# Gate columns of two mixer layers: one f32 product becomes three products of rounded parts, with weights rounded by a converting GpSimd transfer

## The reference, cut to what matters

```python
def hybrid_mixer(h, ...):          # h: 256 x 1024, the normed input
    (aq, ak, av, bq, ...) = jnp.split(h @ w_in, points, axis=-1)
    ya = diff_attention(...); yb = forgetting_attention(...)
    yc = stick_breaking_attention(...); yd = indexed_sparse_attention(...)
    g = jax.nn.sigmoid(h @ w_gate + b_gate).reshape(B, S, 4, D)     # w_gate: 1024 x 4096
    merged = (g[:, :, 0] * (ya @ w_br_a) + g[:, :, 1] * (yb @ w_br_b)
              + g[:, :, 2] * (yc @ w_br_c) + g[:, :, 3] * (yd @ w_br_d))
    return merged @ w_out
```

## Time and profile before

| | us |
|---|---|
| median of 3 runs | 2417.47 |
| lowest, highest | 2414.87, 2417.54 |
| the profiled execution | 2414.68 |
| its span, first to last instruction | 2412.8 |
| PE busy | 2293.6 |
| DVE busy | 1178.6 |
| ACT busy | 1003.7 |
| POOL busy | 297.5 |

### The profile page before, as it was taken

The page is one execution under the profiler, slowest core; times in us unless marked ns, Lnnn a source line. Parts: engine busy times, 40 slices in busy tenths (PEclk is TensorE's granted clock), DMA queues, the critical chain, the costliest instruction groups (busy, mean ns, idle before and its releaser), DMA issues.

```text
span 2412.8 us, 51780 instructions
## 1 busy us (share of the span) xinstructions
PE 2293.6 (95%) x23049; PEld 1925.2 (80%) x23049; DVE 1178.6 (49%) x2070; ACT 1003.7 (42%) x1613; POOL 297.5 (12%) x417
## 2 busy tenths in 40 slices
PE   7999999999999999999999999989999998899876
PEld 7999887889999999887889998468647777786332
DVE  5654544376655654544276655746443455432001
ACT  5434456445444434556444434643124444213111
POOL 0100000031100100000031100046213333200000
PEclk9999999999999999999999999999999999999998
DMA  8754533255655754442346752220111101177997
GB/s 266 244 201 166 175 128 105 88 202 184 213 210 165 255 202 174 165 138 85 110 171 200 241 192 74 105 72 4 41 70 37 39 20 57 34 287 293 420 420 322
DMA packets 207887, 396.61 MB, mean 164 GB/s; under 512 B 9384, under 2 KB 107357, under 8 KB 195245
## 3 DMA queue, kind: packets, MB, share of 16 engines
q1 hardware_dynamic: 205497, 388.79, 45.4%
q0 software_dynamic: 1120, 2.17, 0.3%
q10 hardware_dynamic: 1044, 2.29, 0.3%
HBM read 392.18 MB, written 1.05 MB: 163 GB/s over the span
## 4 chain that ended last, share of the span: by engine, by line
PE 86%; DMA 5%; DVE 3%; ACT 2%; issue 2%; SPq 1%; POOL 0%; ACTq 0%; DVEq 0%
PE ps L284 85%; DMA EX<-in_moe_w_up 3%; DMA RB<-in_moe_w_up 1%; SPq L535 1%; PE ps L1165 0%; DVE wl L462 0%; DVE AR L673 0%; SPq L429 0%; ACT wh L453 0%; DVE AR L1986 0%; PE ps L557 0%; ACT AT L1219 0%; ACT AR L2917 0%; ACT AR L2909 0%; DMA VR<-in_diff_gain 0%
## 5 line engine op out<-in xcount | busy, mean ns | idle before, releaser
L462 DVE TENSOR_TENSOR wl<-RB,wh 128x2048 fp32r<-128x2048 f32 (+5 forms) x189 | 412.5, 2186 | 283.8 <-ACT wh L453 283.3
L284 PE MATMUL ps<-H,RB 128*128 128x256 f32 (+2 forms) x1728 | 451.1, 420 | 2.5 <-ACT AR L2888 1.3
L453 ACT ACTIVATE wh<-RB 128x2048 fp32r<-128x2048 f32 (+5 forms) x189 | 342.5, 1816 | 229.7 <-PE ps L284 201.9
L284 PEld LDWEIGHTS ps<-H,RB 128*128 128x128 f32 (+1 forms) x1728 | 319.6, 189 | 113.2 <-issue 75.2
L284 PE MATMUL ps<-xhf,wl 128*128 128x256 f32 x1408 | 403.0, 286 | 3.0 <-DVE xlf L702 3.0
L284 PE MATMUL ps<-xlf,wh 128*128 128x256 f32 x1408 | 399.6, 284 | 0.0
L284 PE MATMUL ps<-xhf,wh 128*128 128x256 f32 x1408 | 399.5, 284 | 0.0
L284 PE MATMUL ps<-AR 64*64 64x64 f32 (+6 forms) x8536 | 275.8, 232 | 37.8 <-issue 24.6
L284 PEld LDWEIGHTS ps<-AR 64*64 64x64 f32 (+3 forms) x8536 | 250.5, 141 | 72.9 <-issue 61.5
L284 PEld LDWEIGHTS ps<-xhf,wl 128*128 128x128 f32 x1408 | 271.2, 193 | 13.9 <-issue 10.1
L284 PEld LDWEIGHTS ps<-xlf,wh 128*128 128x128 f32 x1408 | 271.4, 193 | 0.1
(11 more groups left out here) (435 smaller groups left out, 3448.5 us busy)
## 6 DMA issues: line engine op xcount, KB each, us to landing
RB<-in_ffn_w_gu SPq DMA_DIRECT2D x88, 1024.0 KB, 7.6
RB<-in_w_in SPq DMA_DIRECT2D x23, 2048.0 KB, 7.8
RB<-in_ffn_w_down SPq DMA_DIRECT2D x16, 2048.0 KB, 7.8
RB<-in_w_gate SPq DMA_DIRECT2D x16, 2048.0 KB, 8.6
RB<-in_ada_w SPq DMA_DIRECT2D x12, 2048.0 KB, 9.7
EX<-in_moe_w_gate SPq DMA_DIRECT2D x22, 1024.0 KB, 19.6
EX<-in_moe_w_up SPq DMA_DIRECT2D x22, 1024.0 KB, 21.7
EX<-in_moe_w_down SPq DMA_DIRECT2D x11, 2048.0 KB, 24.5
```

The costliest lines, as they stand in the source:

```text
L284: return M.matmul(o, lhsT, rhs, start=start, stop=stop, skip_group_check=True)
L453: S.activation(self.pair(h)[0], of(slot_of(*key)), ACT.Copy).then_inc(*did("high", *mark))
L462: V.tensor_tensor(lo, of(slot_of(*key)), hi.bitcast(F32), ALU.subtract).then_inc(*did("low", *mark))
```

## The change

Each gate tile becomes 24 fp32r products in place of 8 f32 products. The parts come in a new way:

- A ring job for the gates is now 256 columns wide (1 MB): the raw weights take the first half of a slot. POOL issues a second transfer of the same weights into the second half, declared fp32r (`RBR` is the ring under that type), which rounds on the way (`rounded`). POOL then subtracts in place: first half = raw - rounded, in 4 pieces of 128x512 (`low`). There are 16 such jobs per layer, 2 gate tiles each, still in a ring of 3.
- The normed input stays in `HB`; ACT rounds it into `UH` at the end of the projections (8 copies), POOL writes the rest into `UL` (8 subtractions).
- PE waits for `gate_low` and `u_low` in place of the landing and `normed`.

```diff
--- before.py
+++ after.py
@@ -367,8 +367,8 @@
             jobs_ffn(2 * l, A["ffn1_w_gu"][l], A["ffn1_w_down"][l])
             for i, (a, b) in enumerate(GROUPS):
                 job(("in", l, i), fill_k(A["w_in"][l], 0, KD, a, b - a), ("low", f"p{l}", 2 * i + 1))
-            for i in range(8):
-                job(("gate", l, i), fill_k(A["w_gate"][l], 0, KD, 512 * i, 512), ("gate", l, 4 * i + 3))
+            for i in range(16):
+                job(("gate", l, i), fill_k(A["w_gate"][l], 0, KD, 256 * i, 256), ("gate", l, 2 * i + 1))
             job(("br_bc", l), fill_two(l), ("branch", l, 1, 7))
             job(("br_d", l), fill_k(A["w_br_d"][l], 0, 2, 0, DM), ("branch", l, 3, 7))
             job(("br_a", l), fill_k(A["w_br_a"][l], 0, 4, 0, DM), ("low", f"b{l}", 1))
@@ -404,6 +404,8 @@
         opened = {3: [("rw_out", 7, 1)], 4: [("rw_out", 7, 1)], 5: [("rw_out", 7, 1)], 6: [("turned", "ya", 1)],
                   7: [("summed", 7)], 8: [("mgate", 1, 7), ("glo", 1)]}
         expert_slots = (3, 4, 5, 8, 6, ring_jobs[0] % NSLOT, (ring_jobs[0] + 1) % NSLOT, (ring_jobs[0] + 2) % NSLOT, 7)
+
+        RBR = sb("RBR", O_RB, [NSLOT, 4096], F32R)
 
         def slot_of(*key):
             return slots[jobs[job_no[key]][2]]
@@ -887,6 +889,9 @@
 
 
 
+        UH = sb("UH", O_H, [KD, T], F32R)
+        UL = sb("UL", W_LOW + 4096, [KD, T], F32R)
+
         def mixer(l, ws, head, behind, then):
             kept = sb(f"kept{l}", STAGE, [13312])
             PQK, SG = view(kept, 0, 2, NK), view(kept, 0, 32, T)
@@ -958,6 +963,10 @@
                         ins = S.activation(out_of(s, lo, hi, 1), ps_of("proj", l, gi, 1, 1)[:, lo - GROUPS[gi][0]:hi - GROUPS[gi][0]],
                                            ACT.Copy, scale=by_row[:, 1:2])
                     ins.then_inc(*did("seg_a", l, gi))
+                    if gi == len(GROUPS) - 1:
+                        for k in range(KD):
+                            AC.wait_ge(*at("normed", l, k))
+                            S.activation(UH[:, k, :], HB[:, k, :], ACT.Copy).then_inc(*did("u_high", l, k))
                     if gi == 5:
                         AC.wait_ge(*at("f_in", l))
                         S.activation(FA, FX, ACT.Abs).then_inc(*did("a"))
@@ -996,7 +1005,7 @@
                         V.tensor_tensor(SPB, FX, FE, ALU.add).then_inc(*did("soft_f", l))
                     if gi == len(GROUPS) - 2:
                         for k in range(KD):
-                            V.scalar_tensor_tensor(out=HA[:, k, :], in0=XT[:, k, :], scalar=vec(g + k), in1=RST,
+                            V.scalar_tensor_tensor(out=HB[:, k, :], in0=XT[:, k, :], scalar=vec(g + k), in1=RST,
                                                    op0=ALU.mult, op1=ALU.mult).then_inc(*did("normed", l, k))
                     for s, nh in turned.get(gi, ()):
                         DV.wait_ge(*at("seg_v", l, gi))
@@ -1079,6 +1088,10 @@
                         YT[rw, dict(b=4, c=6, d=8)[kind] + h // 2, :])
 
 
+            def parts(i):
+                v = RBR[:, jobs[job_no[("gate", l, i)]][2], :]
+                return v[:, 0:2048], v[:, 2048:4096]
+
             behind = {8: [("seg_v", l, 5), ("seg_a", l, 5)], 0: [("rot", l, AT["aq"], 1)], 16: [("rot", l, AT["dq"], 1)],
                       20: [("rot", l, AT["diq"], 1)]}
 
@@ -1119,16 +1132,16 @@
                     if (kind, phase) == ("score", 0):
                         PE.wait_ge(*at("qk_a", l, 20))
                         PE.wait_ge(*at("qk_v", l, 24))
-                        PE.wait_ge(*at("normed", l, 7))
                     if kind == "third":
                         third_pe(h)
                     elif kind == "gate":
-                        i, j = divmod(h, 4)
-                        sv = slot_of("gate", l, i).rearrange("p (k n) -> p k n", k=KD)
-                        PE.wait_ge(*landed("gate", l, i))
+                        i, j = divmod(h, 2)
+                        lo, hi = (x.rearrange("p (k n) -> p k n", k=KD)[:, :, 128 * j:128 * j + 128] for x in parts(i))
+                        PE.wait_ge(*at("gate_low", l, i))
                         ps = bank(("gate", l, h), ("gated", l, h))
                         for k in range(KD):
-                            ins = mm(ps[:, 0:T], sv[:, k, 128 * j:128 * j + 128], HA[:, k, :], k == 0, k == KD - 1)
+                            PE.wait_ge(*at("u_low", l, k))
+                            ins = mm3(ps[:, 0:T], (hi[:, k, :], lo[:, k, :]), (UH[:, k, :], UL[:, k, :]), k == 0, k == KD - 1)
                         ins.then_inc(*did("gate", l, h))
                     elif kind == "score" and phase < 8:
                         q = QKT[64 * (phase % 2):64 * (phase % 2) + 64, 20 + phase // 2, :]
@@ -1281,6 +1294,35 @@
                         DV.wait_ge(*at("weighed", l, kind, h))
                         V.tensor_copy(dst, ps_of("weighed", l, kind, h)[rw, 0:256]).then_inc(*did("y", l, kind, h))
 
+            def gpsimd():
+                def rounded(i):
+                    j = job_no[("gate", l, i)]
+                    slot = jobs[j][2]
+                    PO.wait_ge(*at(*jobs[j - NSLOT][1]))
+                    P.dma_start(parts(i)[1].rearrange("p (k n) -> p k n", k=KD), rows(A["w_gate"][l])[
+                        :, :, 256 * i:256 * i + 256]).then_inc(*did(f"cast{slot}", l, i, by=16))
+
+                def low(i):
+                    lo, hi = parts(i)
+                    PO.wait_ge(*landed("gate", l, i))
+                    PO.wait_ge(*at(f"cast{jobs[job_no[('gate', l, i)]][2]}", l, i))
+                    for x in range(0, 2048, 512):
+                        ins = P.tensor_tensor(lo[:, x:x + 512], slot_of("gate", l, i)[:, x:x + 512],
+                                              hi[:, x:x + 512].bitcast(F32), ALU.subtract)
+                    ins.then_inc(*did("gate_low", l, i))
+
+                rounded(0)
+                rounded(1)
+                PO.wait_ge(*at("proj", l, len(GROUPS) - 1, 1))
+                for k in range(KD):
+                    PO.wait_ge(*at("u_high", l, k))
+                    P.tensor_tensor(UL[:, k, :], HB[:, k, :], UH[:, k, :].bitcast(F32), ALU.subtract).then_inc(
+                        *did("u_low", l, k))
+                for i in range(16):
+                    low(i)
+                    if i + 2 < 16:
+                        rounded(i + 2)
+
             def soften(kind, h):
 
                 mask = SC if kind == "d" else caus
@@ -1368,6 +1410,7 @@
             tensor()
             scalar()
             vector()
+            gpsimd()
```

## The result

| | before | after |
|---|---|---|
| median, us | 2417.51 (4 runs) | 2471.15 (4 runs) |
| lowest, highest | 2414.87, 2418.31 | 2466.57, 2472.63 |
| ratio, 95% interval | | 1.022, 1.0204 to 1.0235 |
| profiled execution, span | 2414.68, 2412.8 | 2466.57, 2465.2 |

I had said 2393, range 2384 to 2434, and 0.30 for slower. The change costs 54 us where I expected 24 us of gain; the time lies above my range.

What follows compares the result with a forecast made beforehand. PE was taken as the bound, busy in 95% of the span. Per layer -14.5 us (saving, first stall, supply) + 2.7 for ACT = -11.8, for two -23.6, from 2414.68 or 2417.47 to 2393; range 2384 to 2434.

Steps and rivals of the forecast that it cites:

- The saving: Gate tiles on PE: 24 products of 0.12 us take 2.88 us per tile, saving 0.57 us, 18.2 us per layer.
- what ACT takes back: Stick-breaking heads, where ACT sets the pace: 5 of 32 tiles' savings lost, 2.7 us per layer, between 0 and 5.
- Rival D: Gate tiles on PE, theory stated after the result: more products of rounded parts save less than thought; no chance given.
- The supply: Gate-weight ring of 3 slots: converting transfer plus POOL's rests just fit; with the first stall, -14.5 us per layer.
- L + T: Gate-weight ring: converting transfer's landing time (11 us) plus POOL's time for the rests (4.7 us); 15.7 us just fits.
- The slower side: Gate-weight ring: converting transfer becomes the bound, landing 16 us after issue gives 2433, 18.6 gives 2467; chance 0.30.
- The start: Before each layer's first gate tile: PE stalls 2.9 us (2.0 to 3.8) for POOL's first rests, ready at 333.9.
- C: Start of the attention stage, theory stated after the result: ACT's eight copies and the start cost the time; no chance given.
- The port of DVE and POOL: Shared SBUF port in the attention stages: DVE has few such operations and 99 of 167 us free; counted as nothing.
- a slower POOL: POOL's rests of gate weights at 8.2 us a pair, with landing in 12: +7 us per layer, within the 0.30 for slower.

Runs made afterwards that it cites:

- the bound run: Changed kernel with no rests of the weights computed (PE reads the rounded half twice) and the input's rests `UL` on DVE; 2389.87 us, ratio 0.9893.

## Why the prediction was wrong, step by step

- **The saving, 18.2 us per layer, and what ACT takes back, 2.7: right.** Without rests the gate tiles' stretch shortens by 16.2 us, so 2.0 are taken back; no run shows by what. Rival D falls.
- **The supply: right in direction, L + T mis-sized on the safe side.** I took L = 11, T = 4.7 and 2 us of issue; the trace shows 8.2, 4.98 and 0.92. POOL's subtractions wait 9.9 us for landings in the whole program, and in these stages PE never for POOL. The slower side that I gave 0.30 rested on this transfer. It got the sign and not the cause: the run without subtractions has every transfer and is 1% faster than before.
- **The start: the wrong engine.** I had POOL's parts ready at 333.9 and counted 2.9 us of stall. POOL's first batch ran from 328.89 for 4.93 us, so it was ready at 333.8. But PE began at 341.6, since DVE's rotations and copies ahead of the transposes' evictions (line 1263) were held out, one POOL instruction at a time (no issue stands directly ahead of these batches):

```profile
325.64 2.70 DVE L1025 TENSOR_TENSOR kept<-kept,SM 128x72 f32<-128x72 f32 x4
...
330.29 2.40 DVE L1257 COPY AT<-kept 128x128 f32<-128x128 f32 x2
```

  The copies take 1.24 us each for 0.22 before. With `UL` still on POOL but no rests, the first tile starts at 336.4; with both off POOL at 330.5. Of the 11.1 us, 5.9 are thus `UL` on POOL with ACT's copies at their place (the part of C that is real; no run splits the two), and 5.2 the first rests.
- **The port of DVE and POOL, where I wrote "I count nothing": the failed step.** I had the row that shows it (0.63 for 0.42 us) and read it as a share lost, by a few operations, on an engine with 99 us to spare. POOL's sum beside it shows a wait instead:

```profile
520.91 0.93 POOL L1486 TENSOR_TENSOR H<-H 128x256 f32<-128x256 f32 x1
```

  It ends at 521.84, and DVE's subtraction, started at 521.49, at 522.12, 0.28 us behind it. The one of 0.42 us, which I called without POOL, starts 0.08 us before another such sum ends (522.68 and 0.92). Among the rivals I put only a slower POOL, and never a kept-out DVE. But DVE's 0.2 to 0.7 us operations in a softmax are links between ACT and PE; free time of DVE elsewhere doesn't pay for them. So PE waits 31.5 us for DVE in the first layer (323 to 523), where it waits 10.1 with the subtractions cut to two columns and 6.7 in the bound run.
- **The clock, which I left out.** Behind such waits PE runs at half speed for a while: 0.50 in the window of 334.5 to 341.6, and 0.90 on the mean of the first layer's gate tiles (341.6 to 511.5), where the bound run has 1.00.

Where the time went, by the gate tiles of the changed kernel against those of the bound run. In the first layer the tiles start 11.1 us later and their stretch is 169.9 - 139.6 = 30.3 us longer. Of the 30.3, the waits for DVE inside it are 21.5 (the four rows above less the one of line 559 and less 2.1 of line 1357, which come behind the last tile) less the 3.8 that the bound run has inside its own, 17.7; the other 12.6 I put down to the clock, an estimate by difference. In the second layer the tiles start 586.4 us after the last of the first, for 575.3, another 11.1, and the stretch is 165.9 us for 139.7, or 26.2. The four differences (11.1, 30.3, 11.1, 26.2) sum to 79 of the 81.1 us between the two spans (2465.2 and 2384.1).

Open: what in POOL makes the block whole behind an issue, and how the start's 5.9 us divide between `UL` on POOL and the place of ACT's copies.

## What to carry to other kernels

Before work is put on an idle GpSimd, list VectorE's operations of the same stretch that read or write SBUF only, and ask who waits for each: price one at what is left of the GpSimd instruction beside it, and at what is left of the whole batch where that stands directly behind an issue; never at a share. If GpSimd must compute behind the issue of a transfer, one wait for the completion of the first piece is cheap (0.3 us in the batch) and gave back 38 us here. Where a subtraction moves to an engine with room, its place in that engine's order decides more than its length: three placements of the same subtractions of 2.28 us gave 2457, 2411 and 2399 us.

## What the runs showed of the hardware that I had not expected

- A VectorE operation on 128x2 elements with all operands in SBUF took 4.56 us beside four back-to-back GpSimd subtractions (4.99 us) directly behind the issue of a transfer, and 0.17 us otherwise. The same batch with no issue ahead, or with one completion waited for, let VectorE in after the piece in execution, as did a pause of 0.45 us between the issue and the batch.
- A GpSimd transfer of 1 MB which rounds f32 to fp32r, in rows of 1 KB, is issued in 0.92 us and lands in 8.2 us at the median, beside a raw one from SP that lands in 5.5.
- After a wait of 7.9 us the fp32r products came at 0.213 us for 0.12, for about 4 us from the first gate tile on.
